# A scan's preparation issued inside the projections ahead of it, and the scan's first units ahead of its remaining token turnings

## The reference

```python
pl = hl @ w_in                                        # latent tokens; the context likewise
xbc = silu(dwconv(p_state[..., :SSD_CONV_DIM], conv_w, conv_b))
dt = softplus(dt_raw + dt_bias)                       # step sizes, 2 directions x 16 heads
# ssd_scan, for each direction; a_neg = -exp(a_log); chunks of 128 tokens
la = dt * a_neg
acum = cumsum(la)                                     # within a chunk
xdt = xs * dt
to_end = exp(acum[-1] - acum)
chunk_decay = exp(acum[-1])
decay = exp(where(causal, acum[l] - acum[s], -inf))
y_diag = einsum(C B^T, decay, xdt)
y_off = einsum(C, carried_state, exp(acum))
# conformer branch: gated input, 31-tap depthwise convolution, layer norm
```

## Time and profile before

| what | value |
|---|---|
| median of 3 runs | 2322.12 us (2322.04 to 2327.14) |
| the profiled execution | 2322.62 us, span 2320.8 us |
| PE busy | 91% of the span |
| DVE busy | 73% |
| ACT busy | 59% |
| POOL busy | 12% |
| mean granted PE clock | 0.96 of full speed |

### The profile page before, as it was taken

How to read it: one execution, slowest core, us unless ns; L and a number is a source line. 1 busy time by engine, 2 the same in 40 slices (tenths; PEclk the granted TensorE clock), 3 DMA queues, 4 the chain that set the end, 5 groups by cost and what they waited for, 6 DMA issues and landing times. The chain is left out here.

```text
span 2320.8 us, 36221 instructions
## 1 busy us (share of the span) xinstructions
PE 2117.6 (91%) x12334; PEld 1737.6 (75%) x12334; DVE 1685.8 (73%) x2810; ACT 1379.7 (59%) x2162; POOL 279.4 (12%) x355
## 2 busy tenths in 40 slices
PE   4999999989998999997899799999699998899995
PEld 3899976679997566666767477787588896677784
DVE  4885544558836579898875599999638774799995
ACT  2664414546636245567654478887558873688884
POOL 0000000000000036455700001110100000011100
PEclk8999999999999999998999799999799997899997
DMA  6455431175552566650012399999332221799993
GB/s 219 162 190 171 144 136 64 45 265 184 185 168 96 215 229 228 229 188 1 2 55 91 110 386 390 386 393 383 125 109 73 82 92 55 288 395 395 394 396 123
DMA packets 127302, 454.97 MB, mean 196 GB/s; under 512 B 13872, under 2 KB 17840, under 8 KB 127024
## 3 DMA queue, kind: packets, MB, share of 16 engines
q1 hardware_dynamic: 116208, 413.14, 48.6%
q0 software_dynamic: 10656, 38.80, 4.5%
q10 hardware_dynamic: 288, 1.05, 0.1%
HBM read 431.97 MB, written 20.97 MB: 195 GB/s over the span
## 5 line engine op out<-in xcount | busy, mean ns | idle before, releaser
L2814 DVE TENSOR_TENSOR moe_w_lo<-ring,moe_w_hi 128x1024 fp32r<-128x1024 f32 x384 | 462.4, 1221 | 49.8 <-ACT moe_w_hi L2746 44.9
L2746 ACT CAST moe_w_hi<-ring 128x1024 fp32r<-128x1024 f32 x384 | 398.8, 1049 | 116.9 <-PE ps L236 109.4
L373 DVE TENSOR_TENSOR ffn_w_lo<-ring,ffn_w_hi 128x1024 fp32r<-128x1024 f32 x132 | 161.0, 1222 | 99.8 <-ACT ffn_w_hi L325 99.6
L325 ACT CAST ffn_w_hi<-ring 128x1024 fp32r<-128x1024 f32 x132 | 137.4, 1044 | 106.0 <-PE ps L236 106.0
L234 PE MATMUL ps<-moe_w_hi,moe_own 128*128 128x512 f32 x480 | 197.3, 411 | 1.3 <-DVE moe_w_lo L2814 0.3
L236 PE MATMUL ps<-moe_w_hi,moe_own 128*128 128x512 f32 x480 | 189.7, 395 | 0.0
L235 PE MATMUL ps<-moe_w_lo,moe_own 128*128 128x512 f32 x480 | 189.6, 395 | 0.0
L234 PE MATMUL ps<-ffn_h_hi,ffn_w_hi 128*128 128x256 f32 x608 | 173.3, 285 | 11.2 <-DVE ffn_w_lo L373 11.2
L235 PE MATMUL ps<-ffn_h_lo,ffn_w_hi 128*128 128x256 f32 x608 | 172.0, 283 | 0.0
L236 PE MATMUL ps<-ffn_h_hi,ffn_w_lo 128*128 128x256 f32 x608 | 172.0, 283 | 0.0
L234 PE MATMUL ps<-even_h_hi,even_w_hi 128*128 128x512 f32 x320 | 131.9, 412 | 11.5 <-DVE even_h_lo L1810 9.0
(11 more groups left out here) (580 smaller groups left out, 5640.0 us busy)
## 6 DMA issues: line engine op xcount, KB each, us to landing
ring<-in_weights SPq DMA_DIRECT2D x766, 512.0 KB, 5.4
expert_rows<-moe_y POOLq DMA_DIRECT2D x30, 512.0 KB, 7.1
token_rows<-moe_token_rows SPq DMA_DIRECT2D x6, 512.0 KB, 3.2
sq<-in_cmp_w SPq DMA_DIRECT2D x1, 2048.0 KB, 7.9
both<-in_x SPq DMA_DIRECT2D x1, 1024.0 KB, 5.7
both<-in_context SPq DMA_DIRECT2D x1, 1024.0 KB, 7.9
expert_rows<-moe_y ACTq DMA_DIRECT2D x2, 512.0 KB, 4.4
out<-both SPq DMA_DIRECT2D x4, 256.0 KB, 2.3
```

The lines of the kernel that those rows point to most:

```text
L325: act.copy(w_hi[:, u % WB], k.slot(act, first + u)).then_inc(w_rounded, 1)
L373: dve.tensor_tensor(w_lo[:, u % WB], k.ring[:, (first + u) % RING], w_hi[:, u % WB], ALU.subtract).then_inc(w_split, 1)
L2746: act.copy(w_hi[:, j % WB].rearrange("p h f -> p (h f)"), k.slot(act, first + GU + j, e).rearrange("p a f -> p (a f)")).then_inc(w_rounded, 1)
L2814: dve.tensor_tensor(w_lo[:, j % WB].rearrange("p h f -> p (h f)"), k.ring[:, (first + GU + j) % RING].rearrange("p a f -> p (a f)"), w_hi[ ...
```

## The change

The preparation is issued inside `even_in` instead of in `ssd`. VectorE takes |dt| behind `step_logs` (m = 3 of the gated pairs) and the masks at m = 0; ScalarE's Exp instructions stand between step 15 and the splits of step 16, its Ln behind those splits; `decay_logs` stands in step 18, TensorE's row sums before step 20, ScalarE's copies in step 21, `low_rows` in step 22, the token sums before step 25, and `ends_of_chunks` in step 26. Two `z` steps take one work item fewer, so 33 instead of 31 are left for the `xbc` steps; all of them, and all pooled taps, now end a step before the last, and the last modulation is kept behind the last convolution. Four taps of tile 7 are moved from `ssd` to `even_in`'s pooled list.

`ssd` starts with two exponentials on ScalarE and two turnings on TensorE, and units 0 and 1 have their fronts between the turnings. The later groups are turned and kept in the loop; `late_taps` is called only in the loop and behind it. The small buffers lie in space that is free at that time; for it the column constants are loaded in two parts, into two buffers.

```diff
-POOLED, ..., LATE_FROM = (2, 4, 5), (0, 1), (3,), 6, 7, 7
+POOLED, ..., LATE_FROM, POOLED_FROM = (2, 4, 5), (0, 1), (3,), 6, 7, 7, 4
-            shared = [(m, j) for m in POOLED for j in cf_order()]
+            shared = [(m, j) for m in POOLED for j in cf_order()] + [(LATE_POOLED, j) for j in cf_order()[:POOLED_FROM]]
# even_in, TensorE
+                    if n == 20:
+                        running_sums()
+                    if n == 25:
+                        token_sums()
# even_in, ScalarE
-                    at, upto = [max(0, len(shared) * (i - FROM) // (NM - FROM)) for i in (n, n + 1)]
+                    at, upto = [max(0, len(shared) * (min(i, NM - 1) - FROM) // (NM - 1 - FROM)) for i in (n, n + 1)]
+                act.wait_ge(dt_abs, 1)
+                act.activation(scan.aneg, col("a_log"), ACT.Exp).then_inc(a_ready, 1)
+                act.activation(flat(scan.la), flat(scan.la), ACT.Exp, scale=-1.0)
                 for m in range(KD):
                     n = 16 + m
                     next_splits(n)
+                    if m == 0:
+                        act.drain()
+                        act.activation(flat(scan.la), flat(scan.la), ACT.Ln, bias=k.ones[:, 0:1]).then_inc(dt_log, 1)
+                    if m == 5:
+                        act.wait_ge(cleared, 1)
+                        act.wait_ge(across, 1)
+                        for d in range(2):
+                            rows = slice(d * ROWS_D, d * ROWS_D + SH)
+                            act.copy(scan.ac_t[rows, :, :]..., k.ps[rows, 6, :]).then_inc(ac_rounded, 1)
# even_in, VectorE
                     first_split(16 + m)
-                    take_taps(1)
+                    take_taps(0 if m in (2, 6) else 1)
                     second_split(16 + m)
+                    if m == 2:
+                        decay_logs()
+                    if m == 6:
+                        low_rows()
                     take_taps(1)
                 for m in range(XBC):
-                    share = -(-len(work) // (XBC - m))
+                    share = -(-len(work) // max(1, XBC - 1 - m))
                     ...
+                    if m == 2:
+                        ends_of_chunks()
+                keep_mods(NM - 1)
# ssd, TensorE
-                for n in range(4):
-                    turn_tokens(n)
-                pe.wait_ge(la_ready, 1)
...
-                pe.wait_ge(kept, FIRST)
-                front(0)
-                front(1)
-                pe.wait_ge(ended, 1)
-                turn_tokens(FIRST)
-                turn_tokens(FIRST + 1)
+                turn_tokens(0)
+                turn_tokens(1)
+                front(0)
+                turn_tokens(2)
+                front(1)
+                for n in range(OPEN - 1, FIRST):
+                    turn_tokens(n)
                 for u in range(NU):
+                    if u < 2:
+                        pe.wait_ge(kept, 3 + u)
+                    if u == SG:
+                        pe.wait_ge(kept, FIRST)
                     back(u)
                     if u + 2 < NU:
                         front(u + 2)
-                    if FIRST + 2 + u < GROUPS:
-                        turn_tokens(FIRST + 2 + u)
+                    if FIRST + u < GROUPS:
+                        turn_tokens(FIRST + u)
# ssd, ScalarE: keeps = [(2, 3), (4, 5), (6, 7), (8,), (9,), (10,), (11,)]
+                keep_tokens(0)
+                keep_tokens(1)
                 for u, (s, d, c, g) in enumerate(units):
                     ...
-                    if FIRST + u < GROUPS:
-                        keep_tokens(FIRST + u)
-                    late_tap(EARLY + u)
+                    if u < len(keeps):
+                        for n in keeps[u]:
+                            keep_tokens(n)
+                    late_tap(POOLED_FROM + u)
# ssd, VectorE
-                late_taps(4)
-                late_taps(5)
-                dve.wait_ge(kept, 3)
+                dve.wait_ge(kept, 2)
                 spread(0)
-                late_taps(2)
                 for u in range(NU):
                     ...
-                    if u % SG == 0 and u // SG + 1 < NU // SG:
-                        dve.wait_ge(kept, GROUPS if u // SG + 1 >= TT else FIRST)
+                    if u % SG == (1 if u < SG else 0) and u // SG + 1 < NU // SG:
+                        if u // SG + 1 in (1, TT):
+                            dve.wait_ge(kept, FIRST - 1 if u < SG else GROUPS)
                         spread(u // SG + 1)
# build_program: a load more in the first stage
-        constants(k, [..., (small[:, :], ins["cols"]),
+            constants(k, [..., (small_first[:, :], ins["cols"][:, 0:n_first]),
+                          (small[:, :], ins["cols"][:, n_first:]),
```

More of the change, by code:

```diff
@@ L1 @@
+from collections import namedtuple
 from contextlib import ExitStack, contextmanager
@@ L134, in norm_vector, with shared_buffers @@
                                  ALU.mult, ALU.mult).then_inc(normed, 1)
-def constants(k, loads):
-    nc = k.nc
+def shared_buffers(k):
     k.ones = k.sb("ones", [P, P])
@@ L146, in constants @@
     k.h = k.sb("h", [P, KD, T2])
+def constants(k, loads):
+    nc = k.nc
     with stage_semaphores(nc, "constants", "loaded", "cleared") as (loaded, cleared), nc.Block(name="constants") as block:
@@ L1536, in tap_parts, with even_in @@
                of[:, part].rearrange("p (r w) -> p r w", r=rows)[:, :, lo + s:w - hi + s])
-def even_in(k, x, col, first_gain, gain, shift, zs, xbc, dt, late_u, cond, padded, mod_bias, mods, weights, gains):
+def even_in(k, x, col, first_gain, gain, shift, zs, xbc, dt, late_u, cond, padded, mod_bias, mods, weights, gains, tri, scan):
     nc = k.nc
@@ L1719, in _ @@
                     next_splits(n)
+                    if m == 0:
[4 more added lines that the diff above has]
+                        act.wait_ge(across, 1)
+                        for d in range(2):
+                            rows = slice(d * ROWS_D, d * ROWS_D + SH)
+                            act.copy(scan.ac_t[rows, :, :].rearrange("p c l -> p (c l)"), k.ps[rows, 6, :]).then_inc(ac_rounded, 1)
                     act.wait_ge(used, done(n))
@@ L1739, in _ @@
             def _(pool):
+                pool.memset(scan.ac_t[:, :, :].bitcast(F32), 0.0)
+                pool.tensor_copy(scan.ident_b[:, :], k.ident[:, :])
+                pool.drain()
+                pool.sem_inc(cleared, 1)
                 pool.wait_ge(h_split, KD)
@@ new lines, in low_rows @@
+                def low_rows():
+                    for d in range(2):
+                        dve.wait_ge(ac_rounded, d + 1)
+                        rows = slice(d * ROWS_D, d * ROWS_D + SH)
+                        low = slice(2 * ROWS_D + d * ROWS_D, 2 * ROWS_D + d * ROWS_D + SH)
+                        lw = dve.tensor_tensor(scan.ac_t[low, :, :].rearrange("p c l -> p (c l)"), k.ps[rows, 6, :],
+                                               scan.ac_t[rows, :, :].rearrange("p c l -> p (c l)"), ALU.subtract)
+                    lw.then_inc(rows_made, 1)
@@ L1860, in _, with ssd @@
                     take_taps(share - share // 2)
-def ssd(k, col, tri, dt, late_u, zs, xbc):
+                keep_mods(NM - 1)
+def ssd(k, col, dt, late_u, zs, xbc, scan):
     nc = k.nc
@@ L3692, in second_block, with kept, by_head @@
             late_u = late[0].rearrange("p (m t) -> p m t", m=2)
-            even_in(k, x, col, col("norm_final"), gains[:, 0, 0], part(0, 0), zs, xbc, dt, late_u, cond, padded, bias, mods, weights, gains)
-            ssd(k, col, tri, dt, late_u, zs, xbc)
+            with ExitStack() as ahead:
+                def kept(name, shape, dtype):
+                    return ahead.enter_context(k.nc.sbuf_tensor(name, shape, dtype))
+                def by_head(at):
+                    return at.rearrange("p (t d h) -> p t d h", t=TT, d=2)
+                size = TT * 2 * SH
+                scan = Decays(by_head(k.sq[:, 6, 0:size]), by_head(k.sq[:, 6, size:2 * size]), k.sq[:, 7, 0:2 * SH],
+                              by_head(rope[:, 0:size]), by_head(col("dt_w")[:, 0:size]), by_head(col("dt_w")[:, size:2 * size]),
+                              kept("never", [P, 2, P], BF16), kept("ident_half", [P, P], BF16),
+                              kept("pick_head", [P, 2, SH], F32R), kept("ac_t", [P, TT, P], F32R))
+                even_in(k, x, col, col("norm_final"), gains[:, 0, 0], part(0, 0), zs, xbc, dt, late_u, cond, padded, bias, mods, weights, gains,
+                        tri, scan)
+                ssd(k, col, dt, late_u, zs, xbc, scan)
         even_out(k, x, col, zs, cf, part(0, 2), late)
```

185 lines of the change are left out of this document (74 added, 111 removed).

## The result

The changed kernel takes 2335.02 us (median of 5 runs, 2331.86 to 2343.07), the kernel before 2322.95 beside it (5 runs). The ratio is 1.0048 [1.0034, 1.0063]: slower by half a per cent, 12 us, above my range (2318 to 2333). The profiled execution of the changed kernel is its median run, 2335.02 us with a span of 2333.3, so the two profiles can be laid beside each other.

The account below looks back on a forecast made before the run. It took TensorE and VectorE to run at one pace in `xbc`, VectorE's backlog ending `even_in`. Terms 0.4 + 5.4 - 5.9 + 3.75 + 1.7 = +5.35 on 2322.62 gave 2328.0, 2327.5 at the median's level; range 2318 to 2333.

Parts of the forecast that it names:

- VectorE in the `xbc` steps: End of `even_in`: two more taps and `ends_of_chunks`, less modulation and waiting, make it +2.05 us (bounds 1 and 4).
- ScalarE's Exp before step 16: Projections: table loads and Exp delay ScalarE's casts, making TensorE late from step 18, +2.4 us (bounds 1.7 and 3.4).
- That rival: ScalarE's table switches: each costs as much again as its load, TensorE 3.8 us later, total 2331.3; chance 0.02.
- Running sums: TensorE in `even_in`: row sums before step 20 delay VectorE's `xbc` start by 0.95 us; token sums cost 0.
- The opening: Scan start: VectorE's first product at 5.0 us instead of 14.6, lead shrinking by unit 5, -5.9 us (bounds -9.6, -3.9).
- the first rival: Opening's lead holds and the projections hide the added work: 2319.7 us, or 2317 with `xbc` work hidden; chance 0.14.
- my signs of being wrong: TensorE not late at step 18, the opening's lead staying above 8 us, or less than 20 pieces left.
- The tail: Scan end: 20 late tap pieces left instead of nine, so the stage ends 3.75 us later (3.4 to 4.6).
- The clock behind it: Start of `even_out`: TensorE's idle time lowers its clock, +1.7 us (bounds 0 and 3.4).
- The first stage: Column constants loaded by two transfers instead of one, costing +0.4 us (bounds 0 and 1.5).
- the others: Rivals: long unit spacing (2331, chance 0.2), dearer table switches (2331.3, 0.02), opening not waiting for the preparation (2331.4, 0.04).

Follow-up runs that it names:

- e10: Kernel before, with each xbc step's scaled taps held until VectorE begins that step's convolution; 2324.83 us, ratio 1.0002.
- e5: Changed kernel, with ScalarE scaling each xbc step's pooled taps only once VectorE has begun that step's convolution; 2332.19 us, ratio 1.0028.
- e4: Kernel before, with five dependent extra VectorE instructions once, ahead of the splits of the first xbc step; 2337.30 us, ratio 1.0064.
- e6: Changed kernel without GpSimd's pooled additions of the xbc steps; 2320.00 us, ratio 0.9987.
- e12: Changed kernel with additions held to the convolution, six tap pieces at the scan's start, tile 7's four taps back in the scan; 2324.87 us, ratio 0.9999.
- e13: Same as e12, with the pooled taps also spread over the steps as before the change; 2321.55 us, ratio 0.9983.
- e14: Same as e13, with Copy in place of ScalarE's two Exp and Ln, so without their table loads; 2320.49 us, ratio 0.9985.
- e3: Changed kernel, with VectorE's 33 taps spread over all 16 xbc steps as before, instead of over 15; 2332.84 us, ratio 1.0044.
- e1: Changed kernel, with ScalarE's scaled taps issued ahead of the wait for the previous convolution and its Silu; 2341.70 us, ratio 1.0081.
- e2: Changed kernel, with six of the twenty tail tap pieces moved into VectorE's wait at the scan's start; 2327.60 us, ratio 1.0025.

## Why the prediction was wrong, step by step

*VectorE in the `xbc` steps* is the step that failed. I added 2.05 us, with bounds of 1 and 4 "as GpSimd may stretch the added taps". It was 10.5. With the additions held to the convolution before and after the change (e10, e5) it is 3.4, inside my bounds; what I left out is that the same work, once late, is stretched by GpSimd. The items themselves were about as large as I said: the last modulation gives back 0.74 us and `ends_of_chunks` costs 1.05. But the added taps were priced at the mean of the earlier trace rows, and that mean holds only at the phase that VectorE and GpSimd had. Even the sentence that my sum went by, "Whatever is added to VectorE in those steps moves the end by its full length", is false: e4 added some 4 us and the end moved by 12.2, the hold of e5 took no work away and gave 5.7, and e6 shows 14.0 us of the part to be GpSimd's doing. The bound should have been what happens when the additions meet splits and taps instead of the convolution. The trace of before had both prices: splits of 0.69 and 1.03 us, and tap groups of four of 1.63 and 3.26 us, in neighbouring steps of the gated part:

```profile
873.92 3.26 DVE L1782 SCALAR_TENSOR_TENSOR h<-sq,cols,h 128x254 f32<-128x254 f32 x4
...
878.20 1.63 DVE L1782 SCALAR_TENSOR_TENSOR h<-sq,cols,h 128x253 f32<-128x253 f32 x4
```

*ScalarE's Exp before step 16.* The size came near, +3.0 us to the first `xbc` tile against 2.4 + 0.95, but by luck. In the changed kernel TensorE doesn't wait at step 18, where I had put the delay; it waits 1.75 us at step 16, ahead of the loads, and that wait goes with the old pace of the pooled taps (e12, e13). Taking the loads out gives back 0.6. Taken by themselves (e13 against e14) the loads are worth 1.7 us, the lower of my bounds. The place of each load and its 1.28 us were as expected, and no extra time at a switch is seen: three loads stand at 893.32, 896.15 and 897.86 within 5.8 us, each with its instruction 1.3 us behind its start. That rival is dead.

*Running sums.* Not taken out by themselves. The row sums' sixteen records stand in the projections at 914.66 and take 1.04 us, as in `ssd`. What e14 has left over the kernel before is 1.4 us, and the forecast's 0.95 fits in it.

*The opening.* Right in mechanism, too small in size: the first product at 4.7 us (I said 5.0), unit 5 at 19.3 instead of 22.0, so 8.6 us of lead and not 5.9. The second product stands at 1073.91, 7.5 us in (I said 9.2), and the four units behind it are 2.9 us apart on the mean, not 3.2. VectorE's last gating of the loop is 9.0 us earlier in the stage than before (110.5 instead of 119.5), so the lead holds to the loop's end, which was half of the first rival. A lead that stays above 8 us was one of my signs of being wrong.

*The tail.* Right: 20 pieces, 8.93 us, 3.8 behind TensorE (forecast 3.75).

*The clock behind it.* Right in mechanism: the sixteen products behind 4.67 us of idle take 10.02 us instead of 7.11, so +2.9, within the bounds of 0 and 3.4, where I took 1.7. No row stands behind the upper bound's 7 us at 1.2 GHz. The same 4.67 us of idle gave 8.80 us in e3 and e5 and 10.15 in e1, so the size varies between executions.

*The first stage.* +0.4 forecast, nothing found: the two issues take 1.61 and 0.43 us instead of 1.52, and the ring's issues behind them take 0.6 us less.

Of the rivals, the first was half right, the lead held, but the projections hid nothing. None of the others had the cause in it; that the range still came within some 2 us is luck: its slow end was made of other costs, and the opening's larger lead took back 3 of the 8.5 us.

What stays open: which instruction of the change first puts VectorE behind in the `xbc` steps, how the lateness keeps itself up from one step to the next, and whether any of the 1.8 us ahead of the projections and the 2.4 from `even_out` on isn't drift between executions.

## What to carry to other kernels

Before adding work to a VectorE that is in step with TensorE, look at what GpSimd does beside it, and price the new work at both phases: with GpSimd's instructions beside operands in PSUM, and beside operands that are both in SBUF. Where a slower neighbour can be tied to the phase that suits it, one semaphore does it (here 5.7 us of 10.5 in this part; in the kernel before, which had the good phase, it cost 1.4). And two delays that an engine sees one after the other are not a sum: take away one alone, then both, before calling either harmless.

## What the runs showed of the hardware that I had not expected

- A 128x512 split on VectorE takes 0.69 us alone and up to 1.24 beside GpSimd's additions; two tap pieces of some 245 columns take 0.82 and up to 1.8. A convolution instruction with one operand in PSUM takes 0.75 in either case (47.76 and 47.67 us for 64).
- GpSimd pays as well: a pair of additions takes 1.23 us beside the convolution and up to 1.8 beside splits and taps.
- The clash feeds itself: with VectorE late once by about 4 us, the part became 12.2 longer (e4).
- 4.67 us of idle on TensorE made the sixteen products behind it 2.9 us longer, at granted clocks of 0.69 and 0.83 over 14 us (1.2 GHz is 0.50, 2.4 GHz 1.00, so these stretches hold both). 1.91 us of idle at the same place left the clock at 1.00 (e2).
